# The first norm of a two-block transformer kernel: the residual is turned with the channel weight alone, and the token's factor is applied behind the projections and the gates

## What is computed

```python
def rmsnorm(x, g):
    y = x32 * lax.rsqrt(jnp.mean(x32 * x32, axis=-1, keepdims=True) + RMS_EPS)
    return (y * g.astype(jnp.float32)).astype(x.dtype)
...
        h = rmsnorm(x, norm_mix[layer])
        proj = h @ w_in[layer]
        qa, ka, va, qb, kb, vb, qi, ki, wi, ga, gb = jnp.split(proj, IN_OFFSETS, axis=-1)
        qa = rope(qa.reshape(B, T, A_HEADS, HEAD_DIM), pos)
...
        merged = jax.nn.sigmoid(ga) * (y_a @ w_up_a[layer]) + jax.nn.sigmoid(gb) * (y_b @ w_up_b[layer])
```

## Time and profile before

| | |
|---|---|
| median of 3 runs | 1170.14 us |
| the runs | 1170.14, 1173.26, 1167.71 us |
| time of the profiled execution | 1168.77 us |
| span of that execution in the trace | 1166.9 us |
| TensorE busy | 992.1 us (85% of the span) |
| GpSimd busy | 878.7 us (75%) |
| VectorE busy | 746.4 us (64%) |
| ScalarE busy | 410.9 us (35%) |
| mean granted clock of TensorE | 0.997 |

### The profile page before, as it was taken

How to read it: one execution, slowest core, us unless ns; L and a number is a source line. 1 busy time by engine, 2 the same in 40 slices (tenths; PEclk the granted TensorE clock), 3 DMA queues, 4 the chain that set the end, 5 groups by cost and what they waited for, 6 DMA issues and landing times.

```text
span 1166.9 us, 13127 instructions
## 1 busy us (share of the span) xinstructions
PE 992.1 (85%) x4298; PEld 657.6 (56%) x4298; DVE 746.4 (64%) x1701; ACT 410.9 (35%) x760; POOL 878.7 (75%) x827
## 2 busy tenths in 40 slices
PE   7999999999999999999997777777777777777775
PEld 6889898788888898798532222222232222222222
DVE  3468332455579778589998666666666666654455
ACT  5446564544433755524222211211221121122131
POOL 5976559799999699477777777777777777777771
PEclk9999999999999999999999999999999999999999
DMA  7643335555555542699999999999999999999997
GB/s 270 211 150 133 109 109 187 183 199 189 181 185 212 179 146 109 234 366 408 396 408 410 409 409 410 410 410 410 410 409 410 409 409 410 409 410 410 409 410 293
DMA packets 89728, 356.81 MB, mean 306 GB/s; under 512 B 9680, under 2 KB 9808, under 8 KB 82384
## 3 DMA queue, kind: packets, MB, share of 16 engines
q0 software_dynamic: 73728, 268.47, 57.9%
q1 hardware_dynamic: 15520, 86.15, 21.1%
q10 hardware_dynamic: 432, 1.57, 0.4%
HBM read 355.10 MB, written 1.05 MB: 305 GB/s over the span
## 4 chain that ended last, share of the span: by engine, by line
PE 38%; POOL 27%; issue 12%; DVE 11%; DMA 8%; ACT 2%; POOLq 1%; DVEq 0%; SPq 0%; ACTq 0%
POOL u_row L2642 14%; POOL v_row L2642 14%; PE bank L890 7%; PE bank L812 5%; DVE u_row L2425 5%; PE bank L726 4%; PE bank L727 4%; PE bank L728 4%; PE bank L892 3%; DMA v_row<-peer_v_dram,expert_of_v 3%; DMA u_row<-peer_u_dram,expert 3%; PE bank L817 2%; PE bank L1181 2%; DMA u_row<-peer_v_dram,expert_of_v 1%; PE bank L900 1%
## 5 line engine op out<-in xcount | busy, mean ns | idle before, releaser
L1308 PE MATMUL bank<-v_row,diag 128*128 128x512 f32 x928 | 427.4, 605 | 145.1 <-DMA v_row<-peer_v_dram,expert_of_v 143.7
L2593 POOL TENSOR_TENSOR w_lo<-raw,w_hi 128x512 fp32r<-128x512 f32 (+1 forms) x280 | 362.6, 1330 | 87.1 <-ACT w_hi L1444 86.0
L2425 DVE CUSTOM_DVE_ANT_0 u_row<-u_row,bank 128x1024 f32<-128x1024 f32 x256 | 301.3, 1216 | 187.7 <-DMA u_row<-peer_u_dram,expert 187.6
L1308 PEld LDWEIGHTS bank<-v_row,diag 128*128 128x128 f32 x928 | 168.4, 190 | 403.7 <-issue 236.8
L2642 POOL DMA_INDIRECT u_row<-peer_u_dram,expert x256 | 244.7, 956 | 97.2 <-issue 71.0
L2642 POOL DMA_INDIRECT v_row<-peer_v_dram,expert_of_v x240 | 229.1, 954 | 73.1 <-issue 69.5
L1714 ACT ACTIVATE diag<-consts,mixw 128x128 f32<-128x128 f32 x256 | 79.6, 389 | 439.7 <-DVE mixw L2440 286.4
L1444 ACT ACTIVATE w_hi<-raw 128x2048 fp32r<-128x2048 f32 x71 | 135.7, 1911 | 78.8 <-PE bank L728 29.0
L890 PE MATMUL bank<-hT_high_and_low,w_hi 128*128 128x512 f32 x352 | 122.2, 394 | 0.6 <-DVE hT_high_and_low L1846 0.6
L892 PE MATMUL bank<-hT_high_and_low,w_lo 128*128 128x256 f32 x352 | 97.5, 277 | 0.0
L890 PEld LDWEIGHTS bank<-hT_high_and_low,w_hi 128*128 128x128 f32 x352 | 66.0, 187 | 16.0 <-issue 0.7
(11 more groups left out here) (292 smaller groups left out, 1445.0 us busy)
## 6 DMA issues: line engine op xcount, KB each, us to landing
raw<-stream_dram SPq DMA_DIRECT2D x74, 1024.0 KB, 4.9
u_row<-peer_u_dram,expert POOLq DMA_INDIRECT x256, 9.9
v_row<-peer_v_dram,expert_of_v POOLq DMA_INDIRECT x240, 10.9
raw_late<-stream_dram SPq DMA_DIRECT2D x3, 1024.0 KB, 4.9
raw_late<-stream_dram SPq DMA_DIRECT2D x4, 512.0 KB, 6.5
residual<-x_in_dram SPq DMA_DIRECT2D x2, 512.0 KB, 4.8
out_dram<-residual SPq DMA_DIRECT2D x4, 256.0 KB, 2.2
consts<-consts_in_dram SPq DMA_DIRECT2D x1, 840.0 KB, 11.9
```

What stands on the lines that cost most here:

```text
L1308: ins = mm(accs[half][:, :], diag[:, 2 * m + i, :], row[:, half * 512:(half + 1) * 512], start=False, stop=True, skip_group_check=True)
L2425: ins = v.tensor_tensor_reduce(out=row_of_u, in0=row_of_u, in1=hn_tile[:, :], scale=1.0, scalar=0.0, op0=ALU.mult, op1=ALU.add, accum_out= ...
L2593: ins = nc.gpsimd.tensor_tensor(w_lo[r][:, cols], source[:, cols], w_hi[r][:, cols].bitcast(F32), ALU.subtract)
```

## The change

It has these parts.

- The turn takes the residual itself (`X`) and not the scaled tokens, so it waits for the tile's transfer and not for the sums. VectorE multiplies by the channel weight as before. The scaling of the tokens (four instructions at L1815) is gone for this norm.
- Tile 0 goes first: its two halves are turned, then four `keep_warm` products follow, then the products of tile 0 with granule qi0, and only then tile 1 is turned (`turned_tokens`). The last four `keep_warm` products of the first norm are gone.
- SyncE issues the 16 KB of channel weights in front, granule qi0 in two halves (columns of chunks 0 and 1, then 2 and 3) with the transfer of tile 1 between them, and the rest of the parameters behind the tables. ScalarE rounds the two halves apart; TensorE waits for the first half ahead of chunk 0 and for the whole ahead of chunk 2.
- The sums of the two tiles stand later on ScalarE.
- The token's factor is applied behind the products: VectorE multiplies the four rope tables by it (two instructions for the two tiles, `scaled`), ScalarE and VectorE apply it in the copies of va, vb and wi, and for the gates, where tokens lie along the free dimension, a row of factors is made: VectorE multiplies the identity by the factor, TensorE multiplies that by a matrix of constants (one new product of 256 columns), and VectorE copies it to `factors`. VectorE now reads each gate's bank and multiplies it by that row (`gate_bank_read`), in place of the copy on ScalarE.

```diff
-    return sorted(pieces) if i == 2 else pieces
+    return sorted(pieces) if i in (0, 2) else pieces
...
-    norm(0)
-    for block in ("qi", "small", "qb"):
+    for t in range(TT):
+        for half in range(2):
+            ps.plan("ST"[half], ("norm", 0, t, half))
+        ps.plan("D", ("qi", t))
+    for block in ("small", "qb"):
...
+        factors = xs[:, 0, 0:T]
...
-            sp.dma_start(X[:, 1, :], x_in[P:2 * P, :]).then_inc(x_in_done[1], 16)
-            load(0)
-            sp.dma_start(params[:, :], params_in).then_inc(consts_done, 16)
+            sp.dma_start(params[:, 0:G_QK], params_in[:, 0:G_QK]).then_inc(gains_done, 16)
+            first, half = slot_source(0)
+            for part, arrived in enumerate((first_part_in, weight_in[0])):
+                cols = slice(half * D + part * 512, half * D + (part + 1) * 512)
+                sp.dma_start(raw[0][:, :].rearrange("p (g n) -> p g n", g=2)[:, :, part * 512:(part + 1) * 512],
+                             stream[first:first + 2, :, cols].rearrange("g p n -> p g n")).then_inc(arrived, 16)
+                if part == 0:
+                    sp.dma_start(X[:, 1, :], x_in[P:2 * P, :]).then_inc(x_in_done[1], 16)
             load(1)
             sp.dma_start(consts[:, P:], consts_in[:, P:]).then_inc(tables_done, 16)
+            sp.dma_start(params[:, G_QK:], params_in[:, G_QK:]).then_inc(consts_done, 16)
             load(2)
...
+                if i == 0:
+                    pe.wait_ge(x_in_done[t], 16)
+                elif i == 1 and half:
                     pe.wait_ge(normed_on_act, t + 1)
                 else:
-                    pe.wait_ge(normed, 2 * TT * i + (3 * t if i == 1 else 2 * t + half) + 1)
+                    pe.wait_ge(normed, 2 * TT * (i - 1) + (3 * t if i == 1 else 2 * t + half) + 1)
                 name = ("norm", i, t, half)
                 bank = ps.start(pe, name)
+                tokens_in = xs if i else X
...
-                    ins = nc.tensor.transpose(bank[:, c * P:(c + 1) * P], xs[:, t, k * P:(k + 1) * P], ident)
+                    ins = nc.tensor.transpose(bank[:, c * P:(c + 1) * P], tokens_in[:, t, k * P:(k + 1) * P], ident)
...
                 def high_products(t):
+                    if before:
+                        before(t)
                     if first:
                         ps.start(pe, outs[t])
                     out = shaped(outs[t])
                     for k, w in zip(chunks, ws[0]):
+                        if name == "qi0" and k == 2:
+                            high_part(name)
                         for x in source:
                             mm(out, x[:, k, t * P:(t + 1) * P], w, start=first and k == chunks[0] and x is source[0], stop=False)
...
-                high_part(name)
+                if name == "qi0":
+                    pe.wait_ge(first_high, 1)
+                else:
+                    high_part(name)
...
-            normed_turn(0)
-            tokens("qi", ("qi0", "qi1"), hT, fresh=0)
+            for half in range(2):
+                turn_piece(0, 0, half)
+            keep_warm(BRIDGE[0][1])
+
+            def turned_tokens(half, t):
+
+                if half == 0 and t == 1:
+                    for part in range(2):
+                        turn_piece(0, 1, part)
+                ps.copied(pe, ("norm", 0, t, half))
+
+            tokens("qi", ("qi0", "qi1"), hT, before=turned_tokens)
             narrow("small", "small", hT, SMALL)
             tokens("qb", ("qb0", "qb1"), hT)
+            pe.wait_ge(tables_done, 16)
+            pe.wait_ge(factors_known, 1)
+            mm(y_bank[:, 0:T], mean_w, xs[:, 1, 0:T], start=True, stop=True).then_inc(factor_rows, 1)
             turn_queries("qi", 0, 1)
...
+            def sums_of_input(t):
+
+                act.wait_ge(x_in_done[t], 16)
+                for half in range(2):
+                    square(X[:, t, half * 512:(half + 1) * 512], t, half, t)
+                    if half == 0:
+                        first_part(t)
+                root_of_sums(t)
...
                         prepare(f"gate{f}")
-                        bank = ps.full(act, ("gate", f))
-                        ps.empty(activation(gates[:, 2 * f:2 * f + 2, :], bank[:, :].rearrange("p (c t) -> p c t", c=2),
-                                            ACT.Copy), ("gate", f))
...
-            norm_sums(0)
-            high_of_norm(0, [0])
+            act.wait_ge(one_done, 1)
+            activation(little[:, 10:11], little[:, 9:10], ACT.Sqrt)
+            halves_of = lambda home: home[0][:, :].rearrange("p (g n) -> p g n", g=2)
+            high_of_norm(0, [(0, 0)])
+            act.wait_ge(first_part_in, 16)
+            activation(halves_of(w_hi)[:, :, 0:512], halves_of(raw)[:, :, 0:512], ACT.Copy).then_inc(first_high, 1)
+            high_of_norm(0, [(0, 1)])
+            act.wait_ge(weight_in[0], 16)
+            activation(halves_of(w_hi)[:, :, 512:1024], halves_of(raw)[:, :, 512:1024], ACT.Copy).then_inc(high_done, 1)
+            prepared[0] = 1
+            sums_of_input(0)
+            high_of_norm(0, [(1, 0), (1, 1)])
             prepare("qi1", 0)
-            high_of_norm(0, [1])
+            sums_of_input(1)
             prepare("qb1")
...
-                ps.empty(activation(va[:, t, :], bank[:, :], ACT.Copy), ("va", t))
+                act.wait_ge(factors_known, 1)
+                ps.empty(activation(va[:, t, :], bank[:, :], ACT.Copy, scale=column(rstd, t)), ("va", t))
...
-            norm(0)
-
+            dve.wait_ge(gains_done, 16)
+            for t in range(TT):
+                for half in range(2):
+                    gain_of_norm(0, half, t)
+                for half in range(2):
+                    low_of_norm(0, half, t)
+            for t in range(TT):
+                norm_scale(t, t + 1)
             dve.wait_ge(tables_done, 16)
+            scaled = consts[:, C_COS:C_ACOS].rearrange("p (w t n) -> p t w n", w=2, t=TT)
+            for t in range(TT):
+                v.tensor_scalar(xs[:, 1, t * P:(t + 1) * P], ident, column(rstd, t), float(CC * P), ALU.mult, ALU.mult)
+                step(v.tensor_scalar(scaled[:, t], scaled[:, t], column(rstd, t), None, ALU.mult))
+            step_done()
+            v.memset(flag[:, :], 0.0).then_inc(factors_known, 1)
...
-                v.tensor_copy(vb[:, t, :], bank[:, HD:2 * HD])
-                v.tensor_copy(wi[:, t, :], bank[:, 3 * HD:SMALL])
+                v.tensor_scalar(vb[:, t, :], bank[:, HD:2 * HD], column(rstd, t), None, ALU.mult)
+                v.tensor_scalar(wi[:, t, :], bank[:, 3 * HD:SMALL], column(rstd, t), None, ALU.mult)
...
+            dve.wait_ge(factor_rows, 1)
+            settle(v.tensor_copy(factors[:, :], y_bank[:, 0:T]))
...
+                    if s and gate_beside(kind, s - 1) is not None:
+                        gate_bank_read(gate_beside(kind, s - 1))
...
+                    gate_bank_read(gate_beside(kind, len(todo)))
...
+            def gate_bank_read(f):
+
+                name = ("gate", f)
+                bank = ps.full(dve, name)
+                ps.empty(v.tensor_tensor(gates[:, 2 * f:2 * f + 2, :], bank[:, :].rearrange("p (c t) -> p c t", c=2),
+                                         row(factors, 2, T), ALU.mult), name)
```

61 lines of the change are left out of this document (20 added, 41 removed).

## The result

| | before | with the change |
|---|---|---|
| median | 1170.48 us (20 runs) | 1173.38 us (20 runs) |
| lowest to highest | 1167.71 to 1173.26 us | 1169.56 to 1176.07 us |
| profiled execution, its span | 1168.77, 1166.9 us | 1172.64, 1170.8 us |

The ratio is 1.0024, with a 95% interval from 1.0016 to 1.0032: the change makes the kernel 2.9 us slower, within 0.5%. I had forecast 1169.5, with a range up to 1173.0. So the result lies just outside, and near the 1172.9 of my first rival.

A forecast was written before the change was run, and what follows sets the result against it. TensorE's pace was taken to bound the kernel to about 500 us, then the gathers, so start gains reach the end. 0.9 - 0.45 + 0.2 = 0.65 us less gave 1169.5 us, range 1165.8 to 1173.0.

The forecast's parts named there:

- first rival: Start: TensorE's low pace lasts through tile 1's products, 3.4 us more, time 1172.9; chance 0.2.
- My sum has the higher level from 11.4 on: Start: TensorE runs at its higher clock from 11.4 us, as the rise came some 4 us after the first instruction before.
- The gain at the start: Start, up to the first low product: 0.9 us less, at most 1.5 us, as GpSimd's low part isn't there before 16.3.
- so I take its landing at 10.3: Transfers: the end of granule qi0 lands at 10.3 us, bounds 10.2 and 11.0, with only 16 KB more ahead of it.
- The new product: TensorE's path: two float32 instructions of 256 columns for the row of factors, a loss of 0.45 us.
- The attentions: Gates' copies leave ScalarE, shortening TensorE's wait before its multiplication by the values: gain 0.2 us, between 0 and 0.5.
- gate1's bank in step 3: Attention: VectorE waits some 1.5 us for this bank before selecting; step 4's scores are 1.8 us late, nothing lost.
- the third rival: Attention A: VectorE sets the end of steps; if reads cost TensorE half their time, 2.8 us, 1172.3; chance 0.07.
- all of its new work had some 1.5: Start: VectorE's two reciprocals and four short multiplications take some 1.5 us, hidden in idle time ahead of its first rotation.
- take as long as plain ones: Attentions: copies of va, vb and wi scaled by the token's factor take no longer than plain copies.
- my sum: Whole kernel: 0.9 at the start, less 0.45 for the product, plus 0.2 in the attentions, 0.65 us less.

The follow-up runs named there:

- t_before: Kernel before, cut off behind the first output projection's residual sum (210 us): median 212.10 us (211.78 to 213.25).
- b_again: Kernel before, unedited, run once more on a chip where runs are longer: 1266.33 us, ratio 1.0008 (0.9983 to 1.0033).
- b_plus1: Kernel before with one call of filling products added ahead of the first turn, on the chip with longer runs: 1265.63 us, ratio 1.0011.
- t_after: Changed kernel, otherwise unedited, cut off behind the first output projection's residual sum: median 213.29 us (212.59 to 215.93).
- t_gates_on_act: Cut changed kernel with the gates' banks copied by ScalarE as before, the token's factor left out of the gates: median 214.03 us (212.7 to 217.47).
- f_third: Whole changed kernel, unedited, again, beside the kernel before (1171.07 us) on one chip: 1172.56 us, ratio 1.0014 (1.0002 to 1.0027).
- a_again: Whole changed kernel, unedited, run once more on a chip where runs are longer: 1267.43 us, ratio 1.0013 (0.9990 to 1.0035).
- t_after_2: Same cut changed kernel as t_after, five more executions on another chip: median 215.69 us (214.74 to 215.88).
- a_plus3: Whole changed kernel with three calls of fillers between chunks 1 and 2 of tile 0, on the chip with longer runs: 1266.19 us, ratio 1.0010.
- t_warm: Cut changed kernel with fillers in all three pauses of the new start (two, three and five calls): median 212.31 us (211.82 to 213.07).
- f_warm: Whole changed kernel with fillers in the three pauses of its start: 1170.96 us beside 1171.41 for the kernel before, ratio 0.9996.
- f_warm_2: f_warm's kernel again, beside the kernel before (1171.07 us) on one chip: 1170.26 us, ratio 0.9992 (0.9981 to 1.0004).
- t_noproduct: t_warm's kernel without the new product that makes the row of factors (gates multiplied by other numbers): median 211.68 us (211.07 to 212.83).
- t_early: Cut changed kernel, tile 1 turned between chunks 1 and 2 of tile 0, sums later, fillers in four pauses: median 212.35 us (211.3 to 212.88).
- f_early: Whole changed kernel with the same edit as t_early: 1171.29 us, ratio 0.9996 (0.9985 to 1.0006) to the kernel before.
- t_nofill: Cut kernel before without the eight calls of filling products of its first norm: median 214.12 us (213.54 to 216.23).

## Why the prediction was wrong, point by point

The profiles together take the start apart. In the table, the landing is the start of ScalarE's last rounding of qi0, the turn that of the index queries, and the sum the start of VectorE's last residual sum (about 205 us). Times in us.

| profile | landing | landing to first low product | low product to turn | turn to sum |
|---|---|---|---|---|
| before, t_before | 10.24, 9.95 | 7.57, 7.53 | 23.85, 23.85 | 163.54, 163.54 |
| b_again, b_plus1 (clock up later) | 10.50, 10.59 | 8.19, 8.21 | 23.85, 23.84 | 163.54, 163.57 |
| after (clock up) | 10.01 | 6.84 | 24.27 | 164.74 (spell) |
| t_after, t_gates_on_act, f_third (clock falls once) | 10.36, 10.34, 10.70 | 7.79, 7.97, 8.03 | 24.27, 24.27, 24.28 | 163.23, 163.57, 163.22 |
| a_again, t_after_2 (down through tile 1) | 10.82, 10.76 | 9.85, 9.67 | 24.67, 24.28 | 163.21, 163.25 |
| a_plus3, t_warm, f_warm, f_warm_2 (fillers) | 11.10, 10.56, 11.58, 11.04 | 6.85, 6.84, 6.84, 6.85 | 24.28, 24.27, 24.27, 24.27 | 163.20, 163.22, 163.21, 163.22 |
| t_noproduct (fillers) | 10.65 | 6.83 | 23.85 | 163.21 |
| t_early, f_early (tile 1 turned earlier, fillers) | 10.21, 11.10 | 6.22, 6.71 | 24.73, 24.38 | 164.76, 164.72 (spells) |
| t_nofill (old order, no fillers) | 10.16 | 7.56 | 23.84 | 165.07 (spell) |

**The step that failed** is "My sum has the higher level from 11.4 on". The sum put the clock at nothing: I had taken the rise of one profile of before as a property of the work, took it to last through the pauses once it was there, and gave the rival 0.2. It held in one of the six profiled executions of the new start without added fillers. In three the clock was up for chunk 0 and fell for 3.4 us (0.95 to 1.2 us more). In two the pace was low through tile 1 (2.8 and 3.0 us more, where the rival had 3.4): in a_again the clock had fallen, in t_after_2 it hadn't risen. The mean over the six is 1.5 us. (The reading of the one profile was off as well, without effect: the pace doubled within the twelve turns at 10.49, which took 2.30 us where the levels give 0.24 or 0.11 each, so nearly 5 us behind the first instruction and not 4.)

The old order lost 0.7 us to the same thing in the two profiles where the clock rose late: its eight fillers ran slowly, at 13.37 in b_again, and the products behind them at full pace. It has 24 products in one block, without a pause, behind its fillers. The change took away the four last `keep_warm` calls and split that block, and I had costed both at nothing and named no work that hides it. Of the two, the split is what the runs point at: in a_plus3 only the pause ahead of chunk 2 is filled, and its one profile has 6.85 us, the same as with all pauses filled. What the four calls count for, no run tells.

The ten executions of t_after and t_after_2 have a mean of 214.71 us, the five of t_before 212.34, the five of t_warm 212.32. So without fillers the new start costs 2.4 us over the start with them, if t_after_2's other chip counts for nothing, and 1.7 us (214.03 less 212.32) on the one chip that t_after and t_warm share. In the whole kernel it is 2.3 us on one chip, where the change cost 2.9 (interval 1.9 to 3.7) in the first comparison and 1.5 in the second. With fillers nothing of the loss is left that these runs could tell from zero, so what they show as its cause is the pace in the pauses of the start. The sizes don't close: the six profiles have a mean of 1.5 us and the executions more, and six profiles are few. That the executions differ, one chip or set of runs more than another, is shown; what decides it within an execution isn't.

**The gain at the start** was forecast as 0.9 us. From landing to low product it is 7.55 - 6.84 = 0.71 us in every profile with the clock up, within 0.02. And it rested on an unchanged landing, "so I take its landing at 10.3". In 13 profiles of the new transfers it lies at 10.01 to 11.58, mean 10.71, and in five of the old ones at 9.95 to 10.59, mean 10.29. The groups overlap, so the 0.4 us that the new transfers seem to cost are likely and not shown. The first profile had the earliest landing of all 13, and so 0.96 us of gain.

**The new product**: 0.45 forecast, 0.42 measured (24.27 less 23.85, and without it 23.85 again; the median fell by 0.6 us, within the scatter and on another chip). **The attentions**: 0.2 forecast, 163.54 - 163.22 = 0.32 measured, and it is the gates: with their copies back on ScalarE it is 163.57 again. VectorE waited 1.69 us for gate1's bank in step 3, as forecast, and nothing was late for it; the third rival is out. Wrong in size, without cost: the scaling of the identity and the tables takes VectorE 4.1 us where all of its new work had some 1.5, from 18.75 to 22.8, and still ends ahead of the rotation at 23.39. And scaled copies don't "take as long as plain ones": ScalarE's copy of va takes 0.69 us in place of 0.60, and VectorE's of vb and wi 0.28 and 0.22 in place of 0.23 and 0.15.

So with the clock up and the landing the same, the change gains 0.71 - 0.42 + 0.32 = 0.61 us, where my sum had 0.65. That kernel exists: it is the one with fillers, and it measured 0.45 and 0.81 us under the kernel before, which two intervals around 1 don't tell from nothing. The arithmetic was right for a kernel other than the one in front of me.

The Trainium skill says ("TensorE: Matmul & The Clock Gate", Part 1: The HAM clock gate) that the number of slow products at the start differs from run to run of the same kernel. The traces agree: t_after and t_after_2 are one kernel, with the clock up at 8.8 us in one and not before the last of the eight products ahead of the low ones at 20.43 in the other (3.56 us for the eight). Had I weighed that sentence, one profile of before would not have fixed the moment of the rise. The rule of Part 4 (PE-mode transpose), the one that I did weigh, isn't borne out: in t_nofill sixteen turns alone, float32 and 128x128, stood ahead of products at full pace.

## What to carry to other kernels

Work that looks useless in a pause can hold the clock for what comes behind, as three calls of fillers ahead of chunk 2 did here; before an edit thins out the start of a kernel, lay out where TensorE pauses, and price the whole stretch at the low clock with the weight of more than one profile. And where a single profiled execution is shorter in the edited stretch and longer elsewhere, take the same kernel again before explaining it: of the two causes that the first pair of profiles offered, one changed sides in the second pair and the other was gone.

## What the runs showed of the hardware

- A steady stream of the same 704 matmuls ran at one of two paces per execution, 346.7 or 353.3 ns a pair, at a granted clock of 1.00 in both. Of the ten profiles of whole kernels, six had the faster (before, a_again, f_warm, f_early, f_third, f_warm_2) and four the slower. It is worth 2.3 us here. In three of the four slower ones (b_again, b_plus1, a_plus3) the granted clock was half from about 209.5 to 213 us, as the stream began, in the fourth and in the six faster ones it wasn't; whether the two belong together isn't shown.
- In the six profiles of the new start without added fillers: where the clock was up before chunk 0 and TensorE then idled for 1.42 to 1.50 us ahead of chunk 2, the granted clock fell to half at 11.2 to 12.1 us, in four of four, for 3.4 us (three) or about 10 (a_again). In the first profile the pace rose within chunk 0, the pause was 0.97 us, and the clock stayed up. In t_after_2 it hadn't risen.
- With three calls of fillers in that pause (0.83 us), which leave it 0.71 to 0.78 us, the clock stayed up in all five profiles that have them. When it first rises fillers don't settle: in f_early, with more of them ahead of chunk 0 than t_after has, the pace was low until past 13 us.
- In attention B the clock fell for 3.4 us at 136 us in four of 18 profiles (after, t_early, f_early, t_nofill), of either order, which costs 1.5 us.
- One chip ran every kernel some 95 us longer than the others, with a mean granted clock of about 0.9; in a_again the clock is 0.99 up to 500 us and 0.84 from 510 us to the end, so the extra time lies behind the stretches that are compared here.
